# Entry of the pa product: operand quarters and weight chunks issued each on its own wait, U3 read first, token sums of the last two pairs kept in a weight block

## What is computed

```python
z = einsum("btd,dn->btn", rms_norm(h), w_in)            # 7 column groups of 2048
xa, sa, vb, gb, sb, ma, mb = split(z)
ya = rg_lru(causal_conv(xa), ...) * silu(sa)            # branch A
pa = einsum("btc,cd->btd", ya, w_proj_a)                # "pa", the stage whose entry is changed
yb = silu(layer_norm(causal_conv(vb * sigmoid(gb)))) * silu(sb)   # branch B
pb = einsum("btc,cd->btd", yb, w_proj_b)
h  = h + einsum("btd,de->bte", sigmoid(ma) * pa + sigmoid(mb) * pb, w_out)
out = rms_norm(h)[:, 16:, :]
```

## Time and profile before

| | us |
|---|---|
| median of 3 runs | 1821.12 |
| lowest and highest | 1820.92, 1823.54 |
| the profiled execution | 1820.43 |
| its span in the trace | 1818.9 |
| PE busy in the span | 1778.0 (98%) |
| DVE busy | 1295.3 (71%) |
| ACT busy | 720.7 (40%) |
| POOL busy | 202.9 (11%) |

### The profile page before, as it was taken

The page is one execution under the profiler, slowest core; times in us unless marked ns, Lnnn a source line. Parts: engine busy times, 40 slices in busy tenths (PEclk is TensorE's granted clock), DMA queues, the critical chain, the costliest instruction groups (busy, mean ns, idle before and its releaser), DMA issues.

```text
span 1818.9 us, 30396 instructions
## 1 busy us (share of the span) xinstructions
PE 1778.0 (98%) x12308; PEld 1665.9 (92%) x12308; DVE 1295.3 (71%) x1585; ACT 720.7 (40%) x960; POOL 202.9 (11%) x211
## 2 busy tenths in 40 slices
PE   8999999999999999999999999999799999999998
PEld 7899999999999999988999999999688899997886
DVE  7969797979798888888677767877423376663431
ACT  6543324242424242423455554554313254443322
POOL 5400000000000000000111211222000112111000
PEclk9999999999999999999999999999899999999999
DMA  5233333333323333254887766674667578847422
GB/s 190 71 111 94 110 95 106 104 98 104 110 92 106 96 105 98 91 162 144 208 224 201 220 150 175 179 204 122 200 234 231 172 206 191 193 143 254 158 86 93
DMA packets 217126, 269.67 MB, mean 148 GB/s; under 512 B 7504, under 2 KB 187856, under 8 KB 215888
## 3 DMA queue, kind: packets, MB, share of 16 engines
q1 hardware_dynamic: 168240, 188.21, 32.2%
q0 software_dynamic: 48800, 80.23, 18.1%
HBM read 227.52 MB, written 40.89 MB: 148 GB/s over the span
## 4 chain that ended last, share of the span: by engine, by line
PE 91%; DVE 4%; DMA 3%; ACT 1%; issue 1%; SPq 0%; POOL 0%; DVEq 0%; ACTq 0%
PE psum L667 51%; PE psum L704 32%; PE psum L858 5%; PE psum L872 2%; DMA raw<-in_w_out 2%; PE psum L764 1%; DVE x_lo L1370 1%; DVE w_lo L1263 1%; DVE region L1690 1%; DMA raw<-in_w_in 0%; DMA t_lo<-gated_a_spill 0%; ACT w_hi L1231 0%; DVE region L1339 0%; DVE w_lo L1804 0%; ACT w_hi L887 0%
## 5 line engine op out<-in xcount | busy, mean ns | idle before, releaser
L667 PE MATMUL psum<-x_hi,w_hi 128*128 128x264 f32 (+1 forms) x1888 | 453.2, 306 | 6.6 <-ACT w_hi L887 3.4
L667 PE MATMUL psum<-x_lo,w_hi 128*128 128x264 f32 (+1 forms) x1888 | 452.0, 306 | 0.0
L667 PEld LDWEIGHTS psum<-x_hi,w_hi 128*128 128x128 f32 x1888 | 306.3, 189 | 22.9 <-issue 5.3
L1285 DVE SCALAR_TENSOR_TENSOR region<-region,conv_cols 128x512 f32<-128x512 f32 x480 | 326.3, 743 | 0.0
L667 PEld LDWEIGHTS psum<-x_lo,w_hi 128*128 128x128 f32 x1888 | 306.3, 189 | 15.0 <-issue 0.2
L887 ACT ACTIVATE w_hi<-raw 128x1024 fp32r<-128x1024 f32 x128 | 135.6, 1059 | 436.7 <-PE psum L667 399.6
L667 PE MATMUL psum<-x_hi,w_lo 128*128 128x264 f32 (+1 forms) x1888 | 291.1, 304 | 2.0 <-DVE w_lo L1263 2.0
L667 PEld LDWEIGHTS psum<-x_hi,w_lo 128*128 128x128 f32 x1888 | 260.2, 188 | 17.3 <-DVE w_lo L1263 2.4
L1263 DVE TENSOR_TENSOR w_lo<-raw,w_hi 128x1024 fp32r<-128x1024 f32 x128 | 161.0, 1258 | 59.0 <-ACT w_hi L887 59.0
L1495 DVE TENSOR_TENSOR w_lo<-region,w_hi 128x1024 fp32r<-128x1024 f32 x87 | 106.4, 1223 | 84.5 <-ACT w_hi L1048 84.4
L1495 DVE TENSOR_TENSOR x_lo<-region,x_hi 128x1024 fp32r<-128x1024 f32 x87 | 106.1, 1223 | 69.7 <-ACT x_hi L1048 68.1
(11 more groups left out here) (223 smaller groups left out, 3234.8 us busy)
## 6 DMA issues: line engine op xcount, KB each, us to landing
raw<-in_w_in SPq DMA_DIRECT2D x140, 512.0 KB, 3.5
region<-in_w_in SPq DMA_DIRECT2D x42, 1024.0 KB, 6.4
raw<-in_w_proj_a SPq DMA_DIRECT2D x32, 512.0 KB, 3.5
region<-in_w_proj_b SPq DMA_DIRECT2D x16, 1024.0 KB, 7.5
raw<-in_w_out SPq DMA_DIRECT2D x32, 512.0 KB, 4.2
region<-in_w_in POOLq DMA_DIRECT2D x21, 512.0 KB, 6.4
sigmoid_spill<-wide POOLq DMA_DIRECT2D x16, 512.0 KB, 5.3
aux<-conv_b_spill POOLq DMA_DIRECT2D x16, 512.0 KB, 5.7
```

What stands on the lines that cost most here:

```text
L667: last = pe.matmul(psum[:, bank, 0:width], weights[:, s, k, m * P:(m + 1) * P], operand[part][:, place(4 * group + k), t0:t0 + width], sta ...
L1285: ins = dve.scalar_tensor_tensor(conv_b[:, t, :], moved, w, conv_b[:, t, :], ALU.mult, ALU.add)
```

## The change

SP issues in the order quarter 0, chunk A0 + 1, quarter 1, chunk A0, quarters 2 and 3, then A0 + 2 and on. Each keeps the wait that protects its place. ACT and DVE cut quarter 0 inside unit 20, at the step where other units cut the next unit's A11, and `read_u3(20)` follows unit 20 directly. The token sums of pairs 6 and 7 go to block 2 of the weight region (free after the unit before last), with a semaphore of their own; so A0 + 1 waits for the spills of pairs 0 to 5 only. `gate_c21(20)` is written one step earlier, with the same instructions around it as before.

```diff
-        t_yb = [raw[:, 1, :]... for h in range(2)]
-        t_yb_last = [... for t in (total[:, :], aux[:, 0:2 * HS])]
+        def t_yb(i):
+            at = raw[:, 1, :].rearrange("p (b n) -> p b n", b=4) if i < PAIRS - 2 else \
+                blocks[:, 2, 4 * (i - PAIRS + 2):4 * (i - PAIRS + 2) + 4, :]
+            return [at[:, 2 * h:2 * h + 2] for h in range(2)]
...
                 elif n == A0 + 1:
-                    sp.wait_ge(yb_t_spilled, 32 * (PAIRS - 1))
+                    sp.wait_ge(yb_t_spilled, 32 * (PAIRS - 2))
...
                 elif h == 0:
                     sp.wait_ge(s4_ready, v - 1)
+                    if v == NX:
+                        sp.wait_ge(yb_t_last_spilled, 64)
...
-            for m in range(4 * PAIRS):
-                load_chunk(A0 + m, ...)
-                if m == 1:
-                    for n in range(4):
-                        load_ya(n)
+            load_ya(0)
+            load_pa(1)
+            load_ya(1)
+            load_pa(0)
+            load_ya(2)
+            load_ya(3)
+            for m in range(2, 4 * PAIRS):
+                load_pa(m)
...
                     elif not last:
                         cut_hi_of(v + 1, A11)
+                    elif v == NX - 1:
+                        ya_cut_hi(0)
...
             for v in range(NX):
                 unit(v)
-            ya_cut_hi(0)
             read_u3(NX - 1)
             for m in range(4 * PAIRS):
-                if m == 1:
-                    gate_c21(NX - 1)
                 chunk_hi(A0 + m)
                 if m < 3:
                     ya_cut_hi(m + 1)
+                if m == 0:
+                    gate_c21(NX - 1)
...
-                    if i < PAIRS - 1:
+                    if i < PAIRS - 2:
                         wait(dve, yb_t_spilled, 32 * i)
                     else:
-                        dve.wait_ge(var_ready, 1)
+                        dve.wait_ge(s4_ready, NX - 1)
...
                     elif not last:
                         cut_lo_of(v + 1, A11)
+                    elif v == NX - 1:
+                        ya_cut_lo(0)
```

More of the change, by code:

```diff
@@ L196, in hybrid_trunk @@
         sums3 = raw[:, 0, :].rearrange("p (k n) -> p k n", k=KH)
-        t_yb = [raw[:, 1, :].rearrange("p (b n) -> p b n", b=4)[:, 2 * h:2 * h + 2] for h in range(2)]
-        t_yb_last = [t.rearrange("p (b n) -> p b n", b=2) for t in (total[:, :], aux[:, 0:2 * HS])]
+        def t_yb(i):
+            at = raw[:, 1, :].rearrange("p (b n) -> p b n", b=4) if i < PAIRS - 2 else \
+                blocks[:, 2, 4 * (i - PAIRS + 2):4 * (i - PAIRS + 2) + 4, :]
+            return [at[:, 2 * h:2 * h + 2] for h in range(2)]
         psum = ctx.enter_context(nc.psum_tensor("psum", [P, 8, 512], F32))
@@ L238, in hybrid_trunk @@
         o_gated, o_spilled = sem("o_gated"), [sem(f"o_spilled{n}") for n in range(2)]
-        sb_silu, yb_ready, yb_t_ready, yb_t_spilled = (
-            sem("sb_silu"), sem("yb_ready"), sem("yb_t_ready"), sem("yb_t_spilled"))
+        sb_silu, yb_ready, yb_t_ready, yb_t_spilled, yb_t_last_spilled = (
+            sem("sb_silu"), sem("yb_ready"), sem("yb_t_ready"), sem("yb_t_spilled"), sem("yb_t_last_spilled"))
         ln_loaded, ln_centred, ln_squared = sem("ln_loaded"), sem("ln_centred"), sem("ln_squared")
@@ L453, in load_operand @@
                     sp.wait_ge(multiplied, B0 - 4 + (S1, S2, S3, A22).index(q) + 1)
-                    sp.wait_ge(yb_t_spilled, 32 * PAIRS)
+                    sp.wait_ge(yb_t_last_spilled, 64)
                 sp.dma_start(token_operand(q)[1].bitcast(F32), yb_spill[spilled_block(q)])\
@@ L465, in _, with load_pa @@
                 load_blocks(v, 1)
-            for m in range(4 * PAIRS):
+            def load_pa(m):
                 load_chunk(A0 + m, w_pa_v[:, 4 * (m % 4):4 * (m % 4) + 4, 256 * (m // 4):256 * (m // 4) + 256])
-                if m == 1:
-                    for n in range(4):
-                        load_ya(n)
+            load_ya(0)
[6 more added lines that the diff above has]
+                load_pa(m)
                 if m == 10:
@@ L553, in spill_t_yb @@
                 pool.wait_ge(yb_t_ready, 2 * i + 2)
-                for h, t in enumerate(t_yb if i < PAIRS - 1 else t_yb_last):
+                for h, t in enumerate(t_yb(i)):
                     b = T_BLOCKS + 2 * h
-                    pool.dma_start(yb_spill[b:b + 2, :, i, :].rearrange("b p n -> p b n"), t).then_inc(yb_t_spilled, 16)
+                    pool.dma_start(yb_spill[b:b + 2, :, i, :].rearrange("b p n -> p b n"), t)\
+                        .then_inc(yb_t_spilled if i < PAIRS - 2 else yb_t_last_spilled, 16)
             def load_ln(dram, i):
@@ L1569, in yb_t_sums @@
                 (r11, r12), (r21, r22) = ([half(o[:, t, :], h) for h in range(2)] for t in range(2))
-                (n1, t3), (t4, t2) = ([t[:, n] for n in range(2)] for t in (t_yb if i < PAIRS - 1 else t_yb_last))
+                (n1, t3), (t4, t2) = ([t[:, n] for n in range(2)] for t in t_yb(i))
                 if not second:
                     dve.wait_ge(yb_ready, i + 1)
-                    if i < PAIRS - 1:
+                    if i < PAIRS - 2:
                         wait(dve, yb_t_spilled, 32 * i)
                     else:
-                        dve.wait_ge(var_ready, 1)
+                        dve.wait_ge(s4_ready, NX - 1)
                     dve.tensor_tensor(n1, r11, r12, ALU.subtract).then_inc(yb_n1_ready, 1)
@@ L1775, in _ @@
             for m in range(4 * PAIRS):
-                if m == 0:
-                    ya_cut_lo(0)
                 chunk_lo(A0 + m)
```

## The result

| | us |
|---|---|
| changed kernel, median of 4 runs (1806.68 to 1811.9) | 1808.38 |
| kernel before, median of 4 runs (1820.92 to 1823.54) | 1821.76 |
| ratio of the two, with its 95% interval | 0.9928 [0.9912, 0.9944] |
| predicted | 1807.8 (1805.0 to 1812.2) |
| profiled execution of the changed kernel, its span | 1806.68, 1805.1 |

The kernel is faster by 0.7%, some 13 us. The two profiled spans differ by 1818.9 - 1805.1 = 13.8 us.

The account below looks back on a forecast made before the run. PE was bound by a 16.3 us wait before A22, made by order on two queues. Landing plus 1274.2 put pa at 1279.9, 13.3 us earlier: 1820.43 becomes 1807.1, plus 0.7 for the median, 1807.8 (1805.0 to 1812.2).

Parts of the forecast that it names:

- SP's order and the landing: SP's queue in unit 20: quarter 0 issued at 1261.2 instead of 1277.21, landing 5.7 us later at 1266.9.
- Rivals A: Quarter 0's load lands faster, in 3.4 to 5.0 us: gain 14.0 to 15.6, time 1805.5 to 1807; chance 0.10.
- B: Quarter 0's load lands late, in 7.5 to 9.8 us: gain 11.5 to 9.2, time 1809.6 to 1811.9; chance 0.12.
- D: ACT's wait for quarter 0 ahead of `read_u2` only moves and grows: slower beyond a 19.0 us landing; chance 0.02.
- The new wait on ACT: Unit 20: quarter 0's cut ahead of `read_u2` delays it from 1264.01 to 1268.7, a new 2.5 us stall before S3.
- the ceiling: Seam into pa: with A22 and S4 unhindered behind S3, pa at 1275.3, 17.8 us earlier, the most to be had.
- DVE's order: Unit 20 on DVE: quarter 0's low part (2.28 us) costs nothing; `read_c22` ends at 1277.0, PE stands 0.9 us before S4.
- The clock: Behind the 2.5 us stall, half clock in S3; loss falls into S4's wait, taken as nothing, up to 3.4 us.
- rival C: Three new PE gaps bring a clock fall reaching A22 and S4: 1.7 to 3.4 us more, 1809.5 to 1811.2; chance 0.15.
- The chunks: pa's start: chunks and quarters 1 to 3 arrive in time, costing nothing while landings stay under about 10 us.
- rival E: pa starts early but starves for late chunks or quarters; 10 us or more lost gives 1817.5 to 1821; chance 0.05.
- Sum: pa's start: 1279.9 instead of 1293.17, 13.3 us less, reaching the end if pa stays dense.

Follow-up runs that it names:

- e1: Changed kernel with quarter 0's cuts on ACT and DVE put back behind unit 20, ahead of `read_u3`; SP's order and sums in block 2 kept: 1803.72 us.
- e4: Changed kernel with pair 6's token sums back in raw, so chunk A0 + 1 waits for their spill; quarter 0 still first on SP: 1819.98 us.
- e2: Changed kernel with both cuts of quarter 0 behind unit 20 and `read_u3` ahead of them: 1803.85 us.
- e7: Changed kernel with pair 7's `gate_rest` and SiLUs on ACT moved behind the high part of chunk A0 + 3: 1806.85 us.
- e5: Changed kernel, but SP issues quarter 0 one product later, after S2 of unit 20 in place of S1: 1812.14 us.
- e6: e2 with pair 7's `gate_rest` and SiLUs on ACT moved behind the high part of chunk A0 + 3: 1803.7 us.
- e3: Kernel before with one swap, `read_u3` ahead of quarter 0's cut on ACT, SP untouched: 1817.52 us.

## Why the prediction was right

Times of the prediction are in the frame of the trace of before; 0.46 is taken off to compare them with the changed kernel's trace.

| step | predicted, less 0.46 | measured |
|---|---|---|
| quarter 0 issued | 1260.7 | 1260.76 |
| its landing | 5.7 us | 5.5 us |
| `read_u2` | 1268.2 | 1268.13 |
| gap ahead of S3 | 2.5 us | 2.21 us |
| `read_u3` | 1272.4, or 1273.2 with the clock's fall | 1272.92 |
| S4 | 1276.6 | 1276.37 |
| pa | 1279.4 | 1279.28 |

**SP's order and the landing.** Right. With the block for the sums it is decisive: e1 shows the gain with these two alone, e4 its loss when A0 + 1 waits again. The order without the block gives next to nothing, and the block without the order was not run. The landing of quarter 0 (KB, us):

```profile
t_lo<-gated_a_spill SPq DMA_DIRECT2D x1, 1024.0 KB, 5.5
```

The nearest row, quarter 3 of before, was 0.2 off, and the seven traces with this order on SP have 5.4 to 5.7 for quarter 0. The fit of the Trainium skill for GpSimd's path ("DMA: Bandwidth & Descriptors", Anatomy of one DMA) gives an estimate of 4.4 for 1 MB; these SP loads took over 1 us longer, so the trace does not agree with it. Rivals A and B fall with it, and D with them: it wanted a landing of 19 us.

**The new wait on ACT.** Right in place and size. That it costs was in the sum from the start: the prediction named 17.8 us as the ceiling and 13.3 as the forecast. e2, with the cut behind `read_u3`, starts pa 17.2 us sooner than the trace of before once the shift is off, 0.6 from the ceiling. So this part of the change is a loss, and the prediction did not ask what leaving it out would give.

**DVE's order.** Right. The low part of quarter 0 cost nothing, and `read_c22` ended when S4 could start:

```profile
1268.26 2.29 DVE L1627 TENSOR_TENSOR t_lo<-t_lo,t_hi 128x2048 fp32r<-128x2048 f32 x1 [6.91 <-ACT t_hi L1186]
...
1275.89 0.41 DVE L1547 TENSOR_TENSOR wide<-aux,psum 128x256 f32<-128x256 f32 x1
```

**The clock, rival C.** The clock did fall, inside S3, and the loss went into the wait for `read_c22`, as the forecast took it:

```profile
1269.00:1270.00 1.00, 1.00 (x11) 1.00 (x10) 1.00 (x1) 1.00 (x3) 0.00 (x0) 1.00 1.05 368
1270.00:1271.00 1.00, 1.00 (x8) 1.00 (x7) 0.67 (x2) 1.00 (x2) 0.00 (x0) 0.52 0.96 306
1271.00:1272.00 1.00, 1.00 (x6) 1.00 (x6) 1.00 (x1) 1.00 (x2) 0.00 (x0) 0.50 0.07 23
```

e7 is the counterproof by luck. Its program is the same up to here, but the clock stayed at 1.00 after a gap of 2.05 us; A22 started 1.1 us sooner (1272.11, shift -0.12), and PE then stood 0.83 us for `read_c22`:

```profile
1268.27 0.39 PE L719 MATMUL psum<-t_hi,w_hi 128*128 128x256 f32 x1 [2.05 <-ACT aux L1099]
1272.11 0.39 PE L719 MATMUL psum<-t_hi,w_hi 128*128 128x256 f32 x1 [0.70 <-ACT aux L1105]
1276.07 0.39 PE L719 MATMUL psum<-x_hi 128*128 128x256 f32 x1 [0.83 <-DVE wide L1547]
```

pa started at 1279.01, within 0.2 us of the changed kernel's time once the shift is off. The fall was worth nothing there. e5 shows the limit of that cover: behind a gap of 5.1 the low clock was worth 1.2 us.

**The chunks: the one step that was wrong.** "All cost nothing" missed 0.8 us, as idle time inside pa's first four chunks, which the prediction had named as a sign of being wrong. Chunk A0 + 2 took 10.1 us to land, just past the "about 10" named as its cover:

```profile
raw<-in_w_proj_a SPq DMA_DIRECT2D x1, 512.0 KB, 10.1
```

It still came in time for its own products. What the step did not list is what stands behind it on ACT, ahead of the cut of A0 + 3:

```profile
1287.62 1.06 ACT L1047 ACTIVATE w_hi<-raw 128x1024 fp32r<-128x1024 f32 x1 [6.86 <-DMA raw<-in_w_proj_a]
1288.58 1.90 ACT L1186 ACTIVATE t_hi<-t_lo 128x2048 fp32r<-128x2048 f32 x1
...
1293.97 1.52 ACT L1139 ACTIVATE aux<-aux,params 128x512 f32<-128x512 f32 x2 [2.97 <-DVE aux L1571]
1295.40 1.99 ACT L1047 ACTIVATE w_hi<-raw 128x1024 fp32r<-128x1024 f32 x2
```

Quarter 3's cut, then SiLUs that wait 2.97 us for DVE, so that A0 + 3's high part is ready at 1296.4, and PE wanted it at 1295.8. It is rival E at a twelfth of its price, and e6 and e7 remove it.

**Sum.** The entry gave 13.43 for 13.3 forecast. That the time came as close, with 13.4 between the medians, is partly luck: the 1.08 given back between pa's start and the next stage, and the 0.99 that came in behind it, cancel, and neither was in the sum. The gap of 1.86 ahead of the next stage is the same in both traces, but the clock fell behind it in the trace of before and not in the changed kernel's. What that is worth can be read off at PE's next wait for `read_u3`, the 0.47 us here, in the trace of before, the changed kernel's and e7's:

```profile
1625.34 0.38 PE L704 MATMUL psum<-t_hi,x_hi 128*128 128x256 f32 x1 [0.47 <-ACT aux L1090]
1612.23 0.38 PE L719 MATMUL psum<-t_hi,x_hi 128*128 128x256 f32 x1 [0.47 <-ACT aux L1105]
1611.18 0.39 PE L719 MATMUL psum<-t_hi,x_hi 128*128 128x256 f32 x1 [0.47 <-ACT aux L1105]
```

From the restart (1472.15, 1459.34 and 1457.99) it is 153.19, 152.89 and 153.19 us. The clock fell in the first and the third. All nine traces fit: 153.19 or 153.18 in the four with a fall (before, e1, e3, e7), 152.88 or 152.89 in the five without. So the 3.4 us at the low clock, which the prediction took as a loss of 1.7, cost 0.30 there. The other 0.69 come in behind that wait, where the nine traces differ by up to 2.5 us (192.87 to 195.33 to the end of the span). No cause is shown for it.

## What to carry to other kernels

When an engine waits for a small reading that takes 0.4 us, look at what stands ahead of that reading in its own queue, and then one queue further: here a transfer whose place had been free for 16 us was held by the wait of another transfer. Give each transfer a place in its queue by the time at which its own wait is met, and free the buffer that makes a neighbour wait. An instruction that waits for a transfer goes behind the readings that PE waits for, and not into the idle time ahead of them: idle time of 3.8 us was no room for a load that lands 2.8 us behind its end and is followed by a cut of 1.8.

## What the runs showed of the hardware

A fall of the granted clock to 1.2 GHz behind a gap of about 2 us is not certain, even with the same gap at the same place. All nine traces have the gap of 1.86 us ahead of the next stage. The clock fell behind it in four (before, e1, e3, e7) and stayed up in five (changed, e2, e4, e5, e6). Here are e7, where it fell, and the changed kernel:

```profile
1458.49:1461.49 3.00, 3.00 (x16) 3.00 (x16) 3.00 (x3) 1.75 (x2) 0.00 (x0) 0.50 0.66 251
```

```profile
1459.34:1460.70 1.36, 1.36 (x11) 1.36 (x12) 1.36 (x2) 1.36 (x2) 0.00 (x0) 1.00 0.94 361
1460.70:1462.20 1.50, 1.50 (x15) 1.50 (x14) 1.50 (x1) 0.90 (x1) 0.00 (x0) 1.00 0.73 276
```

The fall set in 0.2 us behind the restart in e1 and e7, 0.4 in e3 and 1.4 in the trace of before, and lasted 3.4 us in each. Behind gaps of 2.21 and 2.26 us ahead of S3 it fell too (changed, e4), and behind one of 2.05 at the same place it did not (e7).

What a fall costs is set by what else PE would wait for. The 3.4 us at half the clock are 1.7 us of PE's time, but they cost 0.30 us at the next stage and, in the changed kernel's S3, under 0.2.
